# Merged expert up products, and a delta stage with transposes on VectorE

## The reference

```
h = silu(xb @ w1[e]) * (xb @ w3[e])     # 1024 -> 512 hidden columns, twice
y = h @ w2[e]                           # 512 -> 1024
```

```
decay = tril(exp(g_i - g_j));  lmat = strict_tril((kb @ k.T) * decay)      # kb = k * beta
tmat  = inverse(eye + lmat)
u, w  = tmat @ (v * beta),  tmat @ (kb * exp(g));   intra = (q @ k.T) * decay
v_new = u - w @ state;      o = (q * exp(g)) @ state + intra @ v_new
state = state * exp(g_last) + (k * exp(g_last - g)).T @ v_new
```

## Time and profile before

| | us |
|---|---|
| median of three runs | 3272.87 |
| profiled execution | 3270.18 |
| its span, first to last instruction | 3268.1 |
| PE busy in the span | 3064.8 (94%) |
| DVE busy | 1931.4 (59%) |
| ACT busy | 942.3 (29%) |
| POOL busy | 424.4 (13%) |

### The profile page before, as it was taken

One profiled execution on the slowest core, in us unless ns is written; L12 is line 12 of the kernel. 1 busy time (PEld: TensorE's weight loads), 2 busy tenths in 40 slices (PEclk: granted clock), 3 DMA queues, 4 the chain that ended last, 5 costly groups with the idle time before them and its releaser, 6 DMA issues.

```text
span 3268.1 us, 73604 instructions
## 1 busy us (share of the span) xinstructions
PE 3064.8 (94%) x28586; PEld 2326.2 (71%) x28587; DVE 1931.4 (59%) x3796; ACT 942.3 (29%) x1663; POOL 424.4 (13%) x345
## 2 busy tenths in 40 slices
PE   8998999789989999999699979999999799999997
PEld 5446886577765447885577758888778587588886
DVE  1676663556651776673566677664577565576644
ACT  2425110456644334111466640000031622110000
POOL 1000000322231000001222210000155042000000
PEclk9999999899999999999799989999999999999998
DMA  7110324389952212223499922222244000122231
GB/s 290 65 65 15 128 91 155 129 330 379 377 215 96 75 39 78 91 91 135 182 379 374 370 108 89 91 90 91 93 106 101 12 3 3 65 91 91 81 100 65
DMA packets 83203, 443.23 MB, mean 136 GB/s; under 512 B 19480, under 2 KB 19616, under 8 KB 39336
## 3 DMA queue, kind: packets, MB, share of 16 engines
q1 hardware_dynamic: 56488, 381.70, 32.3%
q0 software_dynamic: 23568, 55.62, 4.7%
q10 hardware_dynamic: 2928, 3.07, 0.3%
HBM read 411.00 MB, written 29.23 MB: 135 GB/s over the span
## 4 chain that ended last, share of the span: by engine, by line
PE 87%; ACT 4%; DVE 4%; issue 4%; DVEq 1%; DMA 1%; POOL 0%; ACTq 0%; POOLq 0%; SPq 0%
PE pb L1212 25%; PE pb L793 13%; PE pb L1083 10%; PE pb L944 9%; PE pb L1106 5%; PE pb L984 4%; PE pb L1326 4%; PE pb L1038 3%; PE pb L1593 2%; ACT arena L1621 1%; PE pb L829 1%; PE pb L924 1%; ACT xT L1651 1%; PE pb L1090 1%; PE pb L1469 1%
## 5 line engine op out<-in xcount | busy, mean ns | idle before, releaser
L1212 PE MATMUL pb<-arena,streamed 128*128 128x256 f32 x1952 | 446.8, 381 | 3.6 <-DVE arena L2518 2.8
L1212 PEld LDWEIGHTS pb<-arena,streamed 128*128 128x128 f32 x1952 | 373.7, 192 | 55.8 <-ACT xT L1651 3.2
L1083 PE MATMUL pb<-arena,xT 128*32 x3008 | 350.2, 275 | 17.8 <-issue 11.0
L793 PE MATMUL pb<-xT,streamed 128*128 128x512 f32 x832 | 365.0, 596 | 0.0
L1083 PE MATMUL pb<-streamed,xT 128*32 128x128 f32 x9024 | 352.7, 275 | 6.5 <-issue 6.5
L1083 PEld LDWEIGHTS pb<-arena,xT 128*32 128x32 f32 x3008 | 322.4, 111 | 32.9 <-issue 27.3
L1083 PEld LDWEIGHTS pb<-streamed,xT 128*32 128x32 f32 x9024 | 325.5, 111 | 7.3 <-issue 7.3
L793 PEld LDWEIGHTS pb<-xT,streamed 128*128 128x128 f32 x832 | 156.0, 190 | 196.5 <-issue 196.4
L1761 ACT ACTIVATE streamed<-arena 128x3072 f32 x94 | 260.1, 2767 | 57.0 <-SPq L513 37.2
L1212 PE MATMUL pb<-arena,am 128*128 128x256 f32 x976 | 227.4, 380 | 0.0
L1106 PE MATMUL pb<-arena,am 128*32 x3008 | 184.1, 384 | 26.4 <-issue 21.4
(11 more groups left out here) (497 smaller groups left out, 5380.0 us busy)
## 6 DMA issues: line engine op xcount, KB each, us to landing
arena<-in_w_moe SPq DMA_DIRECT2D x192, 1024.0 KB, 9.3
streamed<-in_w_tail SPq DMA_DIRECT2D x87, 1024.0 KB, 5.0
streamed<-in_w_layer SPq DMA_DIRECT2D x78, 1024.0 KB, 4.9
xT<-xs_dram POOLq DMA_DIRECT2D x22, 512.0 KB, 8.6
ys_dram<-xT POOLq DMA_DIRECT2D x88, 128.0 KB, 9.1
xs_dram<-lnw POOLq DMA_DIRECT2D x12, 512.0 KB, 17.7
arena<-rel_dram SPq DMA_DIRECT2D x8, 448.0 KB, 9.3
lnw<-in_ln_par POOLq DMA_DIRECT2D x3, 1024.0 KB, 7.2
```

The lines of the kernel that those rows point to most:

```text
L793: last = mm(pb[bank][:, 0:cols], unit(w, u, k), rhs[:, k * cols:(k + 1) * cols], start=(k == 0), stop=(k == KC - 1))
L1083: last = mm(pb[m][r0:r0 + MOE_BLOCK, 0:FW], rows, w, start=(k == 0), stop=(k == KC - 1))
L1212: last = mm(pb[p][:, 0:HALF], stat(i), mov(i), start=(opens and i == 0), stop=(closes and i == steps - 1))
```

## The change

In the expert stage the up products of w1 and w3 become one: a matmul streams 256 columns, 128 of each matrix, into one bank, and the stage is split by row chunks instead of by matrix (chunks 0 to 3, then 4 to 7). So the relays are halves by rows too: ACT copies the low half in two instructions, one per matrix, with the silu between; DVE copies the high half. SP loads pieces 0 and 2, then 1 and 3. The silu waits for both halves.

```diff
-                    for m, (relay, relayed) in enumerate(((w1_relay, w1_relayed), (w3_relay, w3_relayed))):
+                    for half, relayed in enumerate((low_relayed, high_relayed)):
                         pe.wait_ge(relayed, l * N_BLK + b + 1)
                         alone(pe)
-                        for k in range(KC):
+                        for k in range(half * STEPS, (half + 1) * STEPS):
...
-                                w = arena[:, bass.ds(off + (m * KC + k) * D_EXP, FW)] if g == 0 else relay[:, (k * (COLS - 1) + g - 1) * FW:(k * (COLS - 1) + g) * FW]
-                                last = mm(pb[m][r0:r0 + MOE_BLOCK, 0:FW], rows, w, start=(k == 0), stop=(k == KC - 1))
+                                if g == 0:
+                                    w = cut(arena[:, bass.ds(off + k * D_EXP, 2 * 2 * PAIR)], 2 * PAIR)[:, :, 0:FW]
+                                else:
+                                    at = (k * (COLS - 1) + g - 1) * FW
+                                    w = cut(up_relay, RELAY)[:, :, at:at + FW]
+                                last = mm(cut(pb[0][r0:r0 + MOE_BLOCK, 0:2 * FW], FW), rows, w, start=(k == 0), stop=(k == KC - 1))
...
                 for b in range(N_BLK):
                     if b + 1 < N_BLK:
                         e = block_expert(act, b + 1)
+                        relay_low(b + 1, e, 0)
                     gate_half(b)
                     if b + 1 < N_BLK:
-                        relay_w1(b + 1, e)
+                        relay_low(b + 1, e, 1)
```

```diff
             def level(c, q):
...
                     if q < LEVELS - 1:
-                        v.tensor_tensor(factor(c, g, 0, 2), factor(c, g, 0, 2), pb[g][:, LW // 2:LW // 2 + LW], ALU.subtract).then_inc(g_tm, 1)
+                        v.tensor_tensor(factor(c, g, 0), factor(c, g, 0), pb[g][:, LW // 2:LW], ALU.subtract).then_inc(g_tm, 1)
...
+                if q < LEVELS - 1:
+                    dve.drain()
+                    for g in range(2):
+                        v.transpose(factor(c, g, 1), factor(c, g, 0)).then_inc(g_tm, 1)
...
+            def rows(m):
+
+                for bank, t in ((3, gbeta), (2, gg)):
+                    for h in range(GH):
+                        spread = t[:, m * GH + h:m * GH + h + 1].to_broadcast([P, P])
+                        out = pb[bank][:].rearrange("p (r h n) -> p r h n", r=2, n=CH)[:, :, h]
+                        last = nc.tensor.transpose(out, spread, identity)
+                last.then_inc(g_front, 1)
...
+            def first_level(m):
+
+                dve.wait_ge(g_exp, 2 * m + 2)
+                if m:
+                    dve.wait_ge(g_lb, (LEVELS - 1) * m)
+                v.scalar_tensor_tensor(out=lbT[0], in0=dT, scalar=-1.0, in1=msk[:, 0:LW], op0=ALU.mult, op1=ALU.mult)
+                dve.wait_ge(g_front, front_done(m, KEY_PRODUCTS))
+                v.tensor_tensor(lT, pb[4][:, 0:LW], dT, ALU.mult).then_inc(g_mats, 1)
+                dve.drain()
+                v.tensor_tensor(lbT[0], pb[4][:, 0:LW], lbT[0], ALU.mult)
+
+            def first_factors(m):
...
+                for g in range(2):
+                    v.tensor_tensor(cut(factor(m, g, 1), CH), ident(GH // 2), cut(lbT[0][:, g * LW // 2:(g + 1) * LW // 2], CH), ALU.add)
+                v.tensor_tensor(dT, dT, incl, ALU.mult)
+                dve.drain()
+                for g in range(2):
+                    last = v.transpose(factor(m, g, 0), factor(m, g, 1))
+                last.then_inc(g_mats, 1)
...
+            def scale_values(m):
+
+                act.wait_ge(g_front, front_done(m, V_TURNED))
+                for h in range(GH):
+                    fn(vB[m % 2][:, h * P:(h + 1) * P], pb[7][:, h * P:(h + 1) * P], ACT.Copy, scale=gbeta[:, m * GH + h:m * GH + h + 1])
...
+            def decay_key_rows(m):
+
+                pool.wait_ge(g_front, front_done(m, KEY_PRODUCTS))
+                x = kbF[m % 2]
+                ptt(x, x, eg, ALU.mult).then_inc(g_rows, 1)
```

More of the change, by code:

```diff
@@ L305, in two_blocks @@
         kbF, qg = ([take(UN * CH) for _ in range(2)] for _ in range(2))
-        dg, db, dT, lT, Am = (take(LW) for _ in range(5))
+        dT, lT, Am = (take(LW) for _ in range(3))
         lbT = [take(LW) for _ in range(LEVELS)]
@@ L1425, in turn_keys @@
                     last.then_inc(g_front, 1)
[L1427 to L1437, removed]
+            def rows(m):
[4 more added lines that the diff above has]
+                        last = nc.tensor.transpose(out, spread, identity)
                 last.then_inc(g_front, 1)
             def key_products(m):
-                for c0, first in ((0, H_K), (LW, H_Q)):
-                    for r, h in UNITS:
-                        last = mm(blk(pb[4], r, h, CH, c0), source(m, H_K, r, h), source(m, first, r, h), start=True, stop=True)
+                pe.wait_ge(g_scaled, m + 1)
+                for r, h in UNITS:
+                    mm(blk(pb[4], r, h), source(m, H_K, r, h), u64(kbF[m % 2], r, h), start=True, stop=True)
+                for r, h in UNITS:
+                    last = mm(blk(pb[4], r, h, CH, LW), source(m, H_K, r, h), source(m, H_Q, r, h), start=True, stop=True)
                 last.then_inc(g_front, 1)
@@ L1527, in _ @@
                 if solve:
[L1528 to L1531 removed]
                     level_product(c, 1)
                 if front:
[L1534 removed]
+                    rows(m)
                 if solve:
@@ L1549, in _ @@
                 if back:
-                    outputs(n, (0, 1))
+                    outputs_of_state(n)
                 if solve:
@@ L1553, in _ @@
                 if back:
-                    outputs(n, (2, 3))
+                    outputs_of_values(n)
                 if solve:
@@ L1799, in _ @@
                 alone(act)
-                relay_w1(0, block_expert(act, 0))
+                e = block_expert(act, 0)
+                for matrix in range(2):
+                    relay_low(0, e, matrix)
                 fn(primed, ones[:, 0:1], ACT.Silu)
@@ L1964, in _ @@
                 if front:
+                    scale_values(m)
+                if solve:
+                    copy_product(c, 3)
+                if front:
                     decays(m)
@@ L1974, in _ @@
                     copy_product(c, 5)
+                if front:
+                    decay_keys(m)
             for h in range(GH):
@@ L2844, in residual @@
                 v.tensor_tensor(resid, vB[n % 2], pb[6][:], ALU.subtract).then_inc(g_rsub, 1)
-            def first_level(c):
-                for g in range(2):
-                    dve.wait_ge(g_up, levels_done(c, 0, g))
-                    v.tensor_tensor(cut(factor(c, g, 0), CH), ident(GH // 2), cut(pb[g][:, LW // 2:LW], CH), ALU.subtract).then_inc(g_tm, 1)
             def level(c, q):
@@ L2942, in _ @@
                 if solve:
-                    level(c, 2)
-                if front:
-                    scale_keys(m)
-                if solve:
                     level(c, 3)
                 if front:
-                    factors(m)
+                    first_level(m)
                 if solve:
```

215 lines of the change are left out of this document (98 added, 117 removed).

## The result

The changed kernel takes 3246.05 us (median of 4 runs, 3245.18 to 3246.93); in the same session the kernel before took 3274.93 (3272.32 to 3281.27), 28.9 more. The ratio is 0.991, with a 95% interval of 0.9896 to 0.9924. The forecast was 3240, range 3208 to 3264. The profiled execution took 3245.18 (span 3243.2), 25.0 less than the profiled execution of before; the forecast had 31 less. Of all the executions reported here one, of run 9, took 4543.69 at a mean granted clock of 0.649, and it is left out of that run's figures.

What follows compares the result with a forecast made beforehand. PE was taken to bound the kernel for nearly the whole span. Expert stage -12, delta stage -25 and clock +6 made -31: 3239, or 3242 at the median's level; forecast 3240, range 3208 to 3264.

Steps and rivals of the forecast that it cites:

- VectorE's tail bounds the delta step: Delta step: PE waits 2.9 for VectorE's 5.9 tail before the state product; step 17.9 instead of 20.35, six steps give 15.
- The transposes: VectorE's tail in the delta step: 0.3 per transpose, four make 1.2, spared from contention with GpSimd.
- The clock: Delta stage: PE's new 2.9 pause drops the clock in half of seven steps, 1.6 each, +6.
- The delta stage's ends: Delta stage outside the six steps: opening gains 3.9, the next stretch 2.8, the last two 3.3.
- Expert stage: Both layers: 6 from wider up products less late starts, 6 from first-turn pauses; -12 in all.
- sixteen rounds make 3.46 where 32 rounds now take some 3.66: Up products of a block, 256 columns instead of 128: 0.2 gained per block, 0.8 per loop turn.
- The lateness: Expert stage: ScalarE's silu and half relay delay the next up products in one of four blocks, 0.3 to 0.75 lost.
- The pauses of the first turn: Expert stage: PE's unexplained pauses, if for fetching instructions, shrink by 3 us per layer, 6 in all (bounds 0 to 16).
- A: Rival, delta stage: VectorE's slow transposes and clock drops take most of the gain; step 20 or more, 3250 to 3262; chance 0.16.
- B: Rival, expert stage: ScalarE's half relay costs 2.76, up starts 1.6 late, 130 lost in all, 3390; chance 0.06.
- C: Rival, both stages: no lateness (-19), no clock drop (-25), all first-turn pauses gone (-16), 3213; chance 0.14.
- D: Rival, expert stage: the weights' transfers bound it and nothing moves there, 3251; chance 0.09.

Runs made afterwards that it cites:

- run 9: run 4's kernel with the expert loop's way back moved between up and down products, slot read ahead of the transpose in all four blocks: 3239.65, ratio 0.9892.
- run 4: Changed kernel with VectorE's mask product and inner product moved behind level 5's subtraction: 3234.01, ratio 0.9876.
- run 6: Changed kernel with the expert's rows split three chunks to five instead of four to four: 3247.0, ratio 0.9923.
- run 7: Changed kernel with both the early slot load of run 5 and the three-to-five row split of run 6: 3246.74, ratio 0.9926.
- run 3: Changed kernel with its up products cut again into 128 columns per matmul, split by rows kept: 3275.2, ratio 0.9998.
- run 5: Changed kernel with the next block's slot read ahead of the hidden rows' transpose in three of four blocks: 3241.83, ratio 0.9901.
- run 11: Changed kernel with run 5's early slot load and the delta stage of run 4: 3231.85, ratio 0.9861.
- run 8: run 4's kernel with the two identity additions also moved ahead of level 4's subtraction: 3235.43, ratio 0.9877.
- run 10: run 8's kernel with the expert loop's way back moved as in run 9: 3237.78, ratio 0.9899.
- run 12: Changed kernel with run 5's early slot load and the delta stage of run 8: 3225.63, ratio 0.9849.
- run 2: Delta stage of the changed kernel with the expert stage of before: 3258.19, ratio 0.995.

## Why the prediction was right, and where it wasn't

The time came out 6 us above the forecast and inside its likeliest case. As a change, 31 was forecast; the medians have 28.9, the two profiles 25.0. Nearly all that is missing in the profiles is missing in the delta stage (13.6 for 19); the expert stage came out by luck. Point by point:

- **VectorE's tail bounds the delta step: shown.** Step 17.96 (said 17.9), PE's part ahead of level 4's update 12.00 (2638.21 to 2650.21, said 12.0), tail 5.96 (2650.21 to 2656.17, said 5.9), pause 2.88 (said 2.9), and run 4 moved it as a tail must move. Within the tail sizes were off and cancelled: additions and mask 2.2 instead of 1.63, against four transposes 1.02 instead of 1.2 and drains and wake-up some 0.1 instead of 0.35.
- **The transposes.** All 80 of them took 0.268 to 0.313, also beside GpSimd's masks (L763, from 2651.57 on), while the additions with two SBUF inputs took 1.25 there and 0.87 before. The Trainium skill (SBUF — State Buffer, "Who interferes with whom") exempts an instruction with a single SBUF input, outside the modes in which VectorE uses two ports, and the trace agrees: none took longer than 0.313. The Trainium skill's 0.311 us for bf16 (VectorE: DVE Perf Modes, "The three transpose paths") lies inside the measured span, here with float32 data.
- **The clock: size right, pattern not foreseen.** 6.7 in three of the six steps and 1.0 in the step behind them (13.59, in runs 6 and 7 without a drop 12.56), said 6. That it came so near is in part luck: in the six steps of the same stage the drops cost 9.4 in runs 3 and 5 and 4.8 in runs 6 and 7. Pauses of 2.88 stand in every step, and only some are followed by a drop; that these pauses matter is shown by runs 4, 9 and 11 (one drop in six steps) and runs 8, 10 and 12 (none).
- **The delta stage's ends: too high.** The opening gave 2.8 (said 3.9), the next stretch 1.2 (said 2.8), the end 3.4 (said 3.3). In the first two the granted clock was 0.76 and 0.81, before 0.91 and 0.96; the clock's term counted the steps alone. The first full step took 19.43, since VectorE's tail makes level 5's subtraction late when there is no state to wait for (PE waits 1.40 for it at 2621.28); no term stood for that. With the clock, 13.6 instead of 19.
- **Expert stage: -12 said, -12.1 measured, by luck: two errors cancel.** The step that failed is "sixteen rounds make 3.46 where 32 rounds now take some 3.66". The 3.66 was a length in the chain that ends with the last matmul's own end; the 3.46 was a pitch. From first start to the next product's start, up took 3.50 before (694.16 to 697.66) and takes 3.47 now (710.22 to 713.69): 0.03 per block, not 0.2. The lateness was also small, 0.5 per turn where the idle time ahead of up rose by about 1.2; the relay was right as a cause, but the slot's load behind a later transpose held up as long (runs 5 to 7). Against both, a pause of 0.5 to 0.7 per turn between up and down went (run 3). Net 0.3 to 0.36 lost per turn, 7.0 from block 8 to the last of both layers, where 6 gained was said.
- **The pauses of the first turn** were taken at 3 per layer with a bound of 8; with the clock spells behind them they gave 10.7 and 9.2, which is what turned the sum (in run 2, with the expert stage of before, the first six blocks of layer 0 took 46.3 instead of 49.3, so the size varies by some 3). That the number of PE's instructions in the loop decides is measured by run 3. That PE fetches instructions in these pauses isn't shown: it is read from the packets of the instruction queue, of which one began in or within 0.8 before each of the three long pauses, but others at times without one.
- **Rivals.** A: half true, the clock but not slow transposes. B: its mechanism is there at a quarter of a microsecond, not 1.4; a half relay costs 1.48, as estimated by elements. C: no, though its loss of all first-turn pauses (-16) is nearest to what went there. D: no, the stage moved.

## What to carry to other kernels

Compare a length only with a length read in the same way: start to start, not a chain's piece against a pitch. When a wait vanishes from a tuned loop, look for the chains that end within a few tenths of it, and shorten all of them or none. When an engine becomes the bound of a step, order its work by who waits for it: moving two products behind the state addition was worth about as much as the whole expert part of the change (3246 to 3234, against 12.1 in the traces).

## What was not expected of the hardware

- A register load behind a waiting instruction isn't free for PE: up started 1.29 after the hidden rows in the changed kernel and 1.33 in run 6, whose relay had ended 0.71 before, but 1.06 in run 7 with the load ahead of the transpose. At the loop's way back PE idled 0.74 ahead of up, and 1.05 and 1.59 in its new place in run 9, with 3.5 us of up products just issued ahead of it.
- VectorE's mask product took 0.42 in the earlier trace rows and in run 8 (2660.55; GpSimd's scaling of the state began 0.10 after it), 0.94 beside GpSimd's masks and 1.84 in run 4, where that scaling had begun 0.33 before; its pair of additions 0.87, 1.25 and 1.78 (run 8). The transposes took 0.268 to 0.314 in both. In run 4:

```profile
2649.74 1.89 POOL L739 TENSOR_TENSOR arena<-arena,egl 128x1024 f32<-128x1024 f32 x1
...
2650.07 1.84 DVE L2934 TENSOR_TENSOR arena<-arena,am 128x256 f32<-128x256 f32 x1
```
